# The first gate and up tiles of a transformer block fed with x times the scale, before the norm and the shift are known

## The chip, the cores and the metric

The kernel runs on one NeuronCore of one Trainium2 chip. The metric is the device time of one execution, in microseconds (us). Of the kernel before three executions were timed.

## The reference, cut to what matters

The reference is a residual block of several sublayers. Only its beginning matters here:

```
mod = (silu(c) @ w_ada + b_ada)            # 9 rows of 1024: shift, scale, gate of three sublayers
h   = rms_norm(x, g_ffn1) * (1 + sc1) + sh1
x   = x + 0.5 * gt1 * (silu(h @ w_gate) * (h @ w_up)) @ w_down
```

x is 512 tokens by 1024 channels in float32, w_ada is 1024 x 9216, the hidden width is 2816 (22 blocks of 128). After this come a mixer (mLSTM and dilated attention), a second feed-forward, and two more layers.

With g = g_ffn1 * (1 + sc1) and r = the reciprocal root of the mean square of a token, the first product is h @ W = r * ((x * g) @ W) + sh1 @ W. The left part needs neither r nor sh1 while TensorE works on it.

## The kernel before

Activations are kept transposed, channels on partitions: `xT` is 8 tiles (kt = 0..7) of 128 channels by 512 tokens. Each engine runs its own written-out program, in the order of the code; semaphores tie them together, and nothing is reordered by a planner.

Every weight tile passes the same pipeline, in a ring of four slots. SyncE loads it into `w_in` (the profile calls it w_stage; `load`, L477). ScalarE rounds it to `w_hi` (`hi`, L797). VectorE forms the remainder `w_lo` (`lo`, L1264) and raises `w_split`. TensorE then does three matmuls for each of the 8 channel tiles (`three`, L2034 to L2036: w_hi by h_hi, w_hi by h_lo, w_lo by h_hi), 24 in all for a tile of 128 outputs. The input h is split in the same way into `h_hi` (ScalarE) and `h_lo` (VectorE). Tiles 0 and 1 are the gate and the up columns of hidden block 0, tiles 2 and 3 those of block 1, and so on.

Before the first such matmul the kernel does this:

- SyncE loads the row of c, an identity, x, twenty small loads of norm weights, biases and `b_ada` (through L472), and then weight tiles 0 and 1; tiles 2 and 3 wait for `ada_done` 14.
- GpSimd loads 16 pieces of w_ada, each 128 rows by 1024 columns (512 KB, L546): 8 for the scale (q = 0), then 8 for the shift (q = 1), into the 8 buffers `ada_w`. Piece 8 + kt waits until VectorE has read piece kt.
- VectorE multiplies each piece by its part of silu(c) and adds it up (`ada_add`, L1274 and L1277). The sum still runs over 128 partitions. TensorE adds those up by 8 one-column matmuls with a vector of ones (`ada_reduce`, L2028), and VectorE adds b_ada (`ada_col`, L1283). `scale_cols` (L1289) then makes g, called `gs`.
- TensorE transposes x (L2001), ScalarE copies it to `xT` (L910) and squares it (L803), TensorE sums the squares (`norm_sum`, L2011), ScalarE makes `rs`, the r above (`norm_rs`, L834 and L836).
- `modulate` makes h: VectorE x * g * r (L1301), ScalarE h_hi with the shift as its bias (L859), VectorE h_lo (L1306).

TensorE's own order is: transposes of x, transposes of the constants' rows (L2005, L2006, which wait for the last small load), norm sums, `ada_reduce(0)`, `ada_reduce(1)`, then `project_pair` on tiles 0 and 1. The rest of w_ada (q = 2..8) is summed by VectorE in between the first feed-forward's tiles.

The second feed-forward and the mixer already begin on x times g, by `lead` (L2045 to L2057): one tile runs on x * g, and 8 one-column matmuls (L2055) multiply the same weights by the shift; VectorE multiplies the result by r afterwards, and the shift's part comes in as a bias.

Of the kernel before, what the change touches and what calls it, by code (L numbers as in the profile page):

```python
# [22 lines left out]
ALU = mybir.AluOpType  # L23
# [139 lines left out]
H_LEAD, H_NORM, H_EVEN, H_ODD = [None, 1, 3], [0, 2, 4], 5, 6  # L163


def read_by_lead(m, k):

    return ([None, 0, 1][m] * (KT - 1)) + k + 1
# [26 lines left out]
def build_program(nc, a, out):  # L195
    ctx = ExitStack()
    with ctx:
# [166 lines left out]
        x_rows = put("x_rows", [P, ST, D])  # L364
        ada_w = sb("ada_w", [P, KT, D])
# [15 lines left out]
        x_t, x_ready, silu_c = sem("x_t"), sem("x_ready"), sem("silu_c")  # L381
# [76 lines left out]
        def _(sp):  # L458
# [20 lines left out]
            def ffn(n):  # L479
                for half in range(2):  # L480
                    t0, f0 = T_FFN[n] + half * 3 * HALF, half * HALF
                    for j in range(2):
                        load(0, t0 + j, cols_of(w_gu[n], f0 * P + j * FF))
                    if t0 == 0:
                        sp.wait_ge(ada_done, 2 * KT - 2)

                    def pair_of_hidden(i):
                        for j in range(4):
                            if n == 1 and isinstance(i, int) and j == 2:
                                sp.wait_ge(shift_sum, 2)  # L490
                            load(i, t0 + 2 + j, cols_of(w_gu[n], i * (2 * P) + (f0 + 1 + j // 2) * P + j % 2 * FF))
# [10 lines left out]
            for n, (what, _, at) in enumerate(IN_TILES):  # L502
# [5 lines left out]
                else:  # L508
                    if n == RING:
                        sp.wait_ge(shift_sum, 1)  # L510
# [27 lines left out]
        def _(pool):  # L538
            pool.memset(rows[:], 0.0).then_inc(zeroed, 1)
            pool.memset(ones[:], 1.0).then_inc(zeroed, 1)  # L540
            pool.memset(eps[:], EPS).then_inc(zeroed, 1)

# [246 lines left out]
        def _(act):  # L789
            act.wait_ge(cols_t, 1)  # L790
            act.activation(cs[:], ps[7][:, 0:KT], ACT.Silu).then_inc(silu_c, 1)
# [35 lines left out]
            def norm_rs(n):  # L827
# [6 lines left out]
                act.activation(rs[:], ps[{0: 0, N_ODD: 3}.get(n, 1)][:], ACT.Ln, bias=eps[:], scale=1.0 / D).then_inc(ln_ready, 1)  # L834
# [16 lines left out]
            def modulate(m, shift):  # L851

                for kt in range(KT):
                    act.wait_ge(hn_ready, m * KT + kt + 1)
                    if m and kt < KT - 1:
                        act.wait_ge(pair_read, read_by_lead(m, kt))
                    elif m:
                        act.wait_ge(w_used, [None, T_MIX, T_FFN[1]][m] + 1)
# [3 lines left out]
            def ffn(n, norm_after, aside=None):  # L862
                for half in range(2):
                    t0, F0 = T_FFN[n] + half * 3 * HALF, (2 * n + half) * HALF

                    def hidden(i, f):


                        led = n == 1 and half == 0 and f == 0
                        for j in range(led, 2):  # L870
                            hi(i, t0 + 2 * f + 2 + j)
                        if led:
                            act.wait_ge(lead_ready, 2)
# [44 lines left out]
            act.wait_ge(gs_ready, 1)  # L918
# [220 lines left out]
            def odd_mixer():  # L1139
# [3 lines left out]
                for kt in range(KT):  # L1143
                    act.wait_ge(hn_ready, 3 * KT + kt + 1)
                    if kt < KT - 1:
                        act.wait_ge(pair_read, 2 * (KT - 1) + kt + 1)
# [104 lines left out]
        def _(dve):  # L1251
# [40 lines left out]
            def modulate(n, m, scale, shift):  # L1292
# [3 lines left out]
                dve.wait_ge(rs_ready, n + 1)  # L1296
                for kt in range(KT + 2):
                    if kt < KT:
                        if kt >= 4:
                            dve.wait_ge(h_ready, H_NORM[m] * KT + kt - 3)  # L1300
                        dve.scalar_tensor_tensor(hn[kt % 4], xT[:, kt], scale[:, kt:kt + 1], rs[:],  # L1301
                                                 ALU.mult, ALU.mult).then_inc(hn_ready, 1)
                    if kt >= 2:
# [22 lines left out]
            def ffn(n, sub, ada, aside=None):  # L1326
                for half in range(2):
                    t0, F0 = T_FFN[n] + half * 3 * HALF, (2 * n + half) * HALF

                    def hidden(i, f, q=None):  # L1330


                        for j in range(n == 1 and half == 0 and f == 0, 2):
# [6 lines left out]
                        dve.tensor_tensor(tmp2[:, f % 2], tmp[:, f % 2], ps[2 * (f % 2) + 1][:], ALU.mult) \  # L1340
                            .then_inc(prod_ready, 1)
# [53 lines left out]
            dve.wait_ge(silu_c, 1)  # L1395
            for q in range(2):
                for kt in range(KT):
                    ada_add(q, kt)
                    if q == 1 and kt == 0:
                        dve.wait_ge(cols_t, 2)  # L1400
                        dve.tensor_copy(cols[:], ps[1][:, 0:N_COLS]).then_inc(cols_ready, 1)
                        dve.wait_ge(cols_t, 3)
                        dve.tensor_copy(bada[:], ps[2][:, 0:72]).then_inc(cols_ready, 1)
                        dve.wait_ge(cols_ready, 2)
# [1237 lines left out]
```

## Time and profile before

| | us |
|---|---|
| median of three runs | 1562.89 (1562.22 to 1563.53) |
| time of the profiled execution | 1567.46 |
| its span, first to last instruction | 1565.8 |
| PE (TensorE matmul) busy | 1481.7 (95%) |
| PEld (TensorE weight load) busy | 1167.9 (75%) |
| DVE (VectorE) busy | 892.3 (57%) |
| ACT (ScalarE) busy | 616.3 (39%) |
| POOL (GpSimd) busy | 384.3 (25%) |
| mean granted TensorE clock | 0.982 of full |

Engines: PE is TensorE, PEld its weight loads, DVE VectorE, ACT ScalarE, POOL GpSimd, SP SyncE. In rows of the profile, `a<-b` is output from input; a float32 matmul that is not rounded to fp32r appears as two MATMUL entries. The profiled execution was 4.57 us longer than the median of the timed ones, and 1.66 us of its time lie outside the span.

### The profile page before, as it was taken

Reading aid. Unit: us, or ns where it says so; the run is one execution under the profiler, and the core shown is the slowest. Engines: PE = TensorE matmul, PEld = TensorE weight load, DVE = VectorE, ACT = ScalarE, POOL = GpSimd, SP = SyncE. Lnnn points to the kernel's source line nnn. Section 1 sums busy time; section 2 is a strip of 40 time slices with the busy share of each in tenths; the row PEclk is TensorE's granted clock in tenths of the full one; section 3 lists DMA queues with packets and bytes.
Section 4 is the critical chain, followed back from the end, with each engine's and each line's share of the span. In section 5 each row is a group of like instructions: output and inputs, shape, how many; then the busy total and the mean of one; then the engine's idle time right before and its main releaser. Section 6 shows DMA issues by size and latency. Waiting matters only on the chain. (4 is left out here: it accounts for less than half of the span.)

```text
span 1565.8 us, 19036 instructions
## 1 busy us (share of the span) xinstructions
PE 1481.7 (95%) x7032; PEld 1167.9 (75%) x7032; DVE 892.3 (57%) x1269; ACT 616.3 (39%) x928; POOL 384.3 (25%) x494
## 2 busy tenths in 40 slices
PE   5999999999999998999999999999899999988977
PEld 3788888888777776468888888888677787766555
DVE  5777436432763676737444344333566357799964
ACT  3422212232533454745342122223431245777634
POOL 3111001000000000040007788200102000999900
PEclk9999999999999999999999999999999999999978
DMA  9888526323242212023433423552133232222201
GB/s 348 269 273 271 198 68 215 94 87 106 70 138 67 81 54 66 1 58 85 121 86 113 138 81 123 160 205 85 54 95 108 68 97 82 81 78 71 68 27 55
DMA packets 204710, 177.93 MB, mean 114 GB/s; under 512 B 7379, under 2 KB 184079, under 8 KB 204118
## 3 DMA queue, kind: packets, MB, share of 16 engines
q1 hardware_dynamic: 188438, 121.87, 26.2%
q0 software_dynamic: 15040, 52.89, 9.6%
q10 hardware_dynamic: 1152, 2.10, 0.4%
q8 instruction: 51, 0.84, 0.2%
q14 instruction: 29, 0.24, 0.1%
HBM read 168.37 MB, written 8.46 MB: 113 GB/s over the span
## 5 line engine op out<-in xcount | busy, mean ns | idle before, releaser
L2034 PE MATMUL ps<-h_hi,w_hi 128*128 128x512 f32 x1224 | 490.7, 401 | 17.0 <-DVE w_lo L1264 11.2
L2036 PE MATMUL ps<-h_hi,w_lo 128*128 128x512 f32 x1224 | 477.9, 390 | 0.0
L2035 PE MATMUL ps<-h_lo,w_hi 128*128 128x512 f32 x1224 | 477.7, 390 | 0.0
L1264 DVE TENSOR_TENSOR w_lo<-w_stage,w_hi 128x1024 fp32r<-128x1024 f32 x225 | 295.3, 1326 | 220.2 <-ACT w_hi L797 217.7
L797 ACT ACTIVATE w_hi<-w_stage 128x1024 fp32r<-128x1024 f32 x225 | 230.7, 1048 | 189.8 <-PE ps L2036 183.4
L2034 PEld LDWEIGHTS ps<-h_hi,w_hi 128*128 128x128 f32 x1224 | 230.2, 188 | 86.1 <-issue 37.0
L2035 PEld LDWEIGHTS ps<-h_lo,w_hi 128*128 128x128 f32 x1224 | 230.5, 188 | 49.1 <-issue 3.6
L2036 PEld LDWEIGHTS ps<-h_hi,w_lo 128*128 128x128 f32 x1224 | 230.3, 188 | 49.2
L2034 PE MATMUL ps<-a_hi,w_hi 128*128 128x512 f32 x544 | 214.4, 394 | 13.1 <-DVE a_lo L1962 9.4
L2035 PE MATMUL ps<-a_lo,w_hi 128*128 128x512 f32 x544 | 212.8, 391 | 0.0
L2036 PE MATMUL ps<-a_hi,w_lo 128*128 128x512 f32 x544 | 212.8, 391 | 0.0
L1340 DVE TENSOR_TENSOR tmp<-tmp,ps 128x512 f32<-128x512 f32 x44 | 30.3, 688 | 197.0 <-PE ps L2036 196.9
L2034 PEld LDWEIGHTS ps<-a_hi,w_hi 128*128 128x128 f32 x544 | 102.8, 189 | 38.2 <-issue 14.0
L879 ACT ACTIVATE a_hi<-tmp 128x512 fp32r<-128x512 f32 (+1 forms) x44 | 27.9, 633 | 234.1 <-DVE tmp L1340 234.1
L2036 PEld LDWEIGHTS ps<-a_hi,w_lo 128*128 128x128 f32 x544 | 102.8, 189 | 21.8
L2035 PEld LDWEIGHTS ps<-a_lo,w_hi 128*128 128x128 f32 x544 | 102.9, 189 | 21.0
L546 POOL DMA_DIRECT2D ada_w<-in_w_ada x72 | 38.7, 539 | 226.6 <-DVE ada_acc L1274 118.9
L781 POOL TENSOR_TENSOR pacc<-pacc,tmp 128x512 f32<-128x512 f32 x49 | 74.4, 1519 | 63.3 <-ACT tmp L1215 59.4
L1277 DVE SCALAR_TENSOR_TENSOR ada_acc<-ada_w,cs,ada_acc 128x1024 f32<-128x1024 f32 x63 | 80.8, 1283 | 9.3 <-DMA ada_w<-in_w_ada 7.3
L1889 DVE SCALAR_TENSOR_TENSOR ps<-gb,cw,ps 128x512 f32<-128x512 f32 x110 | 74.3, 744 | 0.0
L781 POOL TENSOR_TENSOR pacc<-pacc,sq 128x512 f32<-128x512 f32 x48 | 71.9, 1499 | 3.9
L877 ACT ACTIVATE tmp<-ps 128x512 f32<-128x512 f32 x43 | 25.7, 599 | 108.8 <-PE ps L2036 108.8
(435 smaller groups left out, 1502.5 us busy)
## 6 DMA issues: line engine op xcount, KB each, us to landing
w_stage<-in_w_gu SPq DMA_DIRECT2D x88, 512.0 KB, 4.1
ada_w<-in_w_ada POOLq DMA_DIRECT2D x72, 512.0 KB, 6.7
w_stage<-in_w_down SPq DMA_DIRECT2D x44, 512.0 KB, 3.7
w_stage<-in_w_in SPq DMA_DIRECT2D x24, 512.0 KB, 3.9
w_stage<-in_odd_w_in SPq DMA_DIRECT2D x24, 512.0 KB, 3.7
w_stage<-in_even_w_in SPq DMA_DIRECT2D x16, 512.0 KB, 3.9
w_stage<-in_w_out SPq DMA_DIRECT2D x8, 512.0 KB, 3.8
mats<-mats_d POOLq DMA_DIRECT2D x4, 1024.0 KB, 7.0
```

What stands on the lines that cost most here:

```text
L546: pool.dma_start(ada_w[:, kt], a["w_ada"][0][kt * P:(kt + 1) * P, bass.ds(j * D, D)]) \
L781: pool.tensor_tensor(pacc[:, t % 2], pacc[:, t % 2], tap_of[m % 4], ALU.add).then_inc(pool_tap, 1)
L797: act.activation(w_hi[:, c % RING], w_in[:, c % RING], ACT.Copy).then_inc(w_hi_ready, 1)
L877: act.activation(tmp[:, f % 2], ps[2 * (f % 2)][:], ACT.Silu).then_inc(silu_ready, 1)
L879: act.activation(a_hi[:, bass.ds(i * (2 * S) + f * S, S)], tmp2[:, f % 2], ACT.Copy) \
L1264: dve.tensor_tensor(w_lo[:, c % RING], w_in[:, c % RING], w_hi[:, c % RING].bitcast(F32), ALU.subtract).then_inc(w_split, 1)
L1277: dve.scalar_tensor_tensor(acc, ada_w[:, kt], cs[:, kt:kt + 1], acc, ALU.mult, ALU.add).then_inc(ada_done, 1)
L1340: dve.tensor_tensor(tmp2[:, f % 2], tmp[:, f % 2], ps[2 * (f % 2) + 1][:], ALU.mult) \
L1889: dve.scalar_tensor_tensor(acc, gb[:, t % 2, k:k + S], cw[:, t, k:k + 1], acc, ALU.mult, ALU.add).then_inc(tap_done, 1)
L2034: pe.matmul(bank, w_hi[:, slot, k], rhs_hi, start=start, stop=False, skip_group_check=True)
L2035: pe.matmul(bank, w_hi[:, slot, k], rhs_lo, start=False, stop=False, skip_group_check=True)
L2036: return pe.matmul(bank, w_lo[:, slot, k], rhs_hi, start=False, stop=stop, skip_group_check=True)
```

## The change

- The pieces of w_ada for the scale wait for the first two small loads (`c_in`), and the pieces for the shift wait until the last piece of the scale has landed. The loads of weight tiles 0 and 1 wait until piece 5 of the scale has landed, tile 3 until piece 3 of the shift has, tiles 4 and 5 until the shift's matmuls (`shift_sum`) are done.
- VectorE sums only the scale's pieces, then makes `gs`.
- Tiles 0 and 1 run on x * g (`lead_pair`): ScalarE `scaled_hi`, VectorE `scaled_lo`, for each kt.
- The shift's pieces are summed on TensorE (`ada_rows`): float32 matmuls with `cs_wide` as the stationary operand (silu(c) in one column of 32, zeros in the others), four pieces at once in four groups of 32 output partitions, over two halves of 512 columns; 8 matmuls after kt = 3 and 8 after kt = 6. ScalarE copies the two banks to `ada_acc1`; then come `ada_reduce(1)` and 16 one-column matmuls of tiles 0 and 1 with the shift.
- Tiles 2 and 3 run as a pair on the full h. `modulate` runs for them, now while TensorE works on tiles 0 and 1 and after it.
- VectorE multiplies the results of tiles 0 and 1 by r, adds the shift's columns, and the product goes on as before.
- The rest renumbers semaphore values and places; the norm sum moves from bank 0 to bank 3.

The core of the diff:

```diff
+            def ada_rows(first):
+                for kt in range(first, first + 4):
+                    pe.wait_ge(ada_in[kt], 32)
+                for half in range(2):
+                    for g in range(4):
+                        mm = pe.matmul(ps[5 + half][32 * g:32 * g + 32, :], cs_wide[:, first + g],
+                                       ada_w[:, first + g, half * S:(half + 1) * S], start=(first == 0), stop=(first == 4),
+                                       skip_group_check=True)
+                mm.then_inc(ada_done, 4)
+            def lead_pair():
+                for k in range(KT):
+                    pe.wait_ge(h_ready, H_LEAD[0] * KT + k + 1)
+                    for j in range(2):
+                        if k == 0:
+                            pe.wait_ge(w_split, j + 1)
+                        mm = three(ps[j][:], j, k, h_hi[:, k], h_lo[:, k], k == 0, k == KT - 1)
+                        if k == KT - 1:
+                            mm.then_inc(w_used, 1)
+                    if k < KT - 1:
+                        mm.then_inc(pair_read, 1)
+                    if k == 3:
+                        ada_rows(0)
+                    if k == 6:
+                        ada_rows(4)
+                ada_reduce(1)
+                pe.wait_ge(mod_ready, 2)
+                for j in range(2):
+                    for k in range(KT):
+                        mm = pe.matmul(ps[7][:, KT + j:KT + j + 1], w_in[:, j, k], sublayer(0)[1][:, k:k + 1],
+                                       start=(k == 0), stop=(k == KT - 1))
+                mm.then_inc(shift_sum, 1)
...
             ada_reduce(0)
-            ada_reduce(1)
...
# GpSimd
-            for q in range(2):
-                for kt in range(KT):
-                    ada_load(q, ADA_ORDER[q], kt)
+            pool.wait_ge(c_in, 32)
+            for kt in range(KT):
+                ada_load(0, ADA_ORDER[0], kt)
+            pool.wait_ge(ada_in[KT - 1], 16)
+            for kt in range(KT):
+                ada_load(1, ADA_ORDER[1], kt)
# ScalarE
-            for c in range(2):
-                hi(0, c)
+            hi(0, 0)
+            act.wait_ge(gs_ready, 1)
+            scaled_hi(0, gs)
+            hi(0, 1)
+            for kt in range(1, KT):
+                scaled_hi(kt, gs)
             norm_rs(0)
+            hi(0, 2)
+            act.wait_ge(ada_done, 2 * KT)
+            for half in range(2):
+                act.activation(ada_acc1[:, half * S:(half + 1) * S], ps[5 + half][:], ACT.Copy).then_inc(c_ready, 1)
+            hi(0, 3)
             act.wait_ge(mod_ready, 2)
# VectorE, after the scale's ada_add, cols, bada and ada_col(0)
+            lo(0, 0)
+            scaled_lo(H_LEAD[0], 0, gs)
+            lo(0, 1)
+            for kt in range(1, KT):
+                scaled_lo(H_LEAD[0], kt, gs)
             modulate(0, 0, *sublayer(0))
+            dve.wait_ge(shift_sum, 1)
+            link(dve.tensor_copy(rcol[:, 0:2], ps[7][:, KT:KT + 2]))
+            dve.wait_ge(h_ready, (H_NORM[0] + 1) * KT)
+            dve.tensor_tensor(tmp[:, 0], ps[0][:], rs[:], ALU.mult).then_inc(lead_ready, 1)
+            dve.wait_ge(sq_used, KT)
+            dve.tensor_tensor(sq[:, 0], ps[1][:], rs[:], ALU.mult).then_inc(lead_ready, 1)
```

In `modulate` on VectorE, for this sublayer alone, `lo(0, 2)` stands ahead of the first x * g * r, and `ada_col(1)` and `lo(0, 3)` stand after the third; in the first hidden block no weight tile is split, so tiles 4 and 5 are split in the second.

## Rows read from the trace of the kernel before

**Rows 1.** The page, busy time of each engine over the span.
```profile
PE 1481.7 (95%) x7032; PEld 1167.9 (75%) x7032; DVE 892.3 (57%) x1269; ACT 616.3 (39%) x928; POOL 384.3 (25%) x494
```

**Rows 2.** Timeline of PE: start, duration, operation, idle before it and its releaser.
```profile
14.23 6.06 PE L2001 MATMUL ps<-ident,x_rows 128*128 128x128 f32 x32 [10.47 <-DMA x_rows<-in_x]
20.78 0.31 PE L2005 MATMUL ps<-ident,rows 103*128 103x103 f32 x1 [0.50 <-DMA rows<-in_b_ada]
...
20.99 7.90 PE L2011 MATMUL ps<-sq,ones 128*128 128x512 f32 x16
28.73 1.84 PE L2028 MATMUL ps<-ones,ada_acc 128*128 128x1 f32 x16
34.80 3.57 PE L2028 MATMUL ps<-ones,ada_acc 128*128 128x1 f32 x16 [4.23 <-DVE ada_acc L1277]
41.70 0.76 PE L2034 MATMUL ps<-h_hi,w_hi 128*128 128x512 f32 x1 [3.33 <-DVE h_lo L1306]
```

**Rows 3.** Timeline of DVE, the first 70 us.
```profile
21.02 1.28 DVE L1277 SCALAR_TENSOR_TENSOR ada_acc<-ada_w,cs,ada_acc 128x1024 f32<-128x1024 f32 x1 [0.24 <-DMA ada_w<-in_w_ada]
...
30.61 0.17 DVE L1283 TENSOR_TENSOR mod<-ps,bada 128x8 f32<-128x8 f32 x1 [0.62 <-PE ps L2028]
...
34.67 2.35 DVE L1264 TENSOR_TENSOR w_lo<-w_stage,w_hi 128x1024 fp32r<-128x1024 f32 x2
38.41 0.17 DVE L1283 TENSOR_TENSOR mod<-ps,bada 128x8 f32<-128x8 f32 x1 [1.39 <-PE ps L2028]
...
47.43 2.08 DVE L1306 SCALAR_TENSOR_TENSOR h_lo<-tmp,mod,h_hi 128x512 fp32r<-128x512 f32 x3
49.42 2.36 DVE L1264 TENSOR_TENSOR w_lo<-w_stage,w_hi 128x1024 fp32r<-128x1024 f32 x2
...
66.01 0.69 DVE L1340 TENSOR_TENSOR tmp<-tmp,ps 128x512 f32<-128x512 f32 x1 [1.54 <-PE ps L2036]
```

**Rows 4.** Windows of all engines: us, busy and count of PE, PEld, DVE, ACT, POOL, clock, DMA share, GB/s.
```profile
32.00:34.00 2.00, 0.00 (x0) 0.00 (x0) 1.82 (x2) 0.90 (x1) 0.00 (x0) 0.68 0.90 261
...
1553.70:1555.00 1.30, 1.30 (x12) 1.30 (x12) 0.00 (x0) 0.47 (x1) 0.00 (x0) 1.00 0.00 0
1555.20:1556.00 0.80, 0.80 (x4) 0.72 (x4) 0.00 (x0) 0.00 (x0) 0.00 (x0) 0.50 0.00 0
```

**Rows 5.** Windows of PE alone: us, busy and count, granted clock, DMA share, GB/s.
```profile
41.70:46.40 4.70, 4.70 (x11) 0.50 1.04 390
54.80:59.50 4.70, 4.70 (x22) 1.00 0.18 50
```

**Rows 6.** DMA queues from 5 to 13 us: packets, MB, share.
```profile
q1 hardware_dynamic: 496, 2.03, 62.5%
q0 software_dynamic: 361, 1.29, 39.8%
```

**Rows 7.** DMA queues from 14 to 31 us.
```profile
q0 software_dynamic: 1604, 5.84, 88.8%
q1 hardware_dynamic: 1604, 0.77, 15.6%
```

**Rows 8.** Timeline of ACT, the first 60 us.
```profile
25.69 0.61 ACT L910 ACTIVATE xT<-ps 128x512 f32<-128x512 f32 x1
...
31.84 1.06 ACT L797 ACTIVATE w_hi<-w_stage 128x1024 fp32r<-128x1024 f32 x1 [4.12 <-DMA w_stage<-in_w_gu]
...
55.85 0.63 ACT L879 ACTIVATE a_hi<-tmp 128x512 fp32r<-128x512 f32 x1 [0.88 <-DVE tmp L1340]
```

**Rows 9.** Groups of PE by line: count, busy us, mean ns, idle before.
```profile
L2508 PE MATMUL ps<-gb,dgc 128*128 128x512 f32 x34 | 14.9, 592 | 0.0
...
L2055 PE MATMUL ps<-mod,w_stage 128*128 128x1 f32 x16 | 1.8, 245 | 0.0
```

**Rows 10.** Timeline of PE in the attention.
```profile
646.46 1.95 PE L2302 MATMUL ps<-pt_a,va 128*64 128x256 f32 x16
```

More of the change, by code:

```diff
@@ L364, in build_program @@
         x_rows = put("x_rows", [P, ST, D])
+        put = region(at_of["a_lo"] + KT * S * 4, S * 4)
+        cs_wide = put("cs_wide", [P, KT, 32])
         ada_w = sb("ada_w", [P, KT, D])
@@ L509, in _ @@
                     if n == RING:
-                        sp.wait_ge(shift_sum, 1)
+                        sp.wait_ge(shift_sum, 2)
                     load(0, T_MIX + n, cols_of(a["w_in"][0], at))
@@ L541, in _ @@
             pool.memset(eps[:], EPS).then_inc(zeroed, 1)
+            pool.memset(cs_wide[:], 0.0).then_inc(zeroed, 1)
             def ada_load(q, j, kt):
@@ L833, in norm_rs @@
                     act.wait_ge(sq_used, SUMMED[n])
-                act.activation(rs[:], ps[{0: 0, N_ODD: 3}.get(n, 1)][:], ACT.Ln, bias=eps[:], scale=1.0 / D).then_inc(ln_ready, 1)
+                act.activation(rs[:], ps[{0: 3, N_ODD: 3}.get(n, 1)][:], ACT.Ln, bias=eps[:], scale=1.0 / D).then_inc(ln_ready, 1)
                 act.wait_ge(ln_ready, n + 1)
@@ L866, in hidden @@
                     def hidden(i, f):
-                        led = n == 1 and half == 0 and f == 0
-                        for j in range(led, 2):
+                        led = half == 0 and f == 0
+                        for j in range([2, 1][n] if led else 0, 2):
                             hi(i, t0 + 2 * f + 2 + j)
                         if led:
-                            act.wait_ge(lead_ready, 2)
+                            act.wait_ge(lead_ready, [1, 4][n])
                             act.activation(tmp[:, 0], tmp[:, 0], ACT.Silu, bias=rcol[:, 0:1]).then_inc(silu_ready, 1)
@@ L1296, in modulate @@
                 dve.wait_ge(rs_ready, n + 1)
+                if n == 0:
+                    lo(0, 2)
                 for kt in range(KT + 2):
@@ L1302, in modulate @@
                                                  ALU.mult, ALU.mult).then_inc(hn_ready, 1)
+                    if n == 0 and kt < 2:
+                        continue
+                    if n == 0 and kt == 2:
+                        ada_col(1, ADA_ORDER[1])
+                        lo(0, 3)
+                        dve.wait_ge(mod_ready, 2)
                     if kt >= 2:
@@ L1330, in hidden @@
                     def hidden(i, f, q=None):
-                        for j in range(n == 1 and half == 0 and f == 0, 2):
+                        led = half == 0 and f == 0
+                        for j in range([2, 1][n] if led else 0, 2):
                             lo(i, t0 + 2 * f + 2 + j)
@@ L1967, in _ @@
             modulate(2, 2, *sublayer(2))
-            dve.wait_ge(shift_sum, 2)
+            dve.wait_ge(shift_sum, 3)
             link(dve.tensor_copy(rcol[:, 0:1], ps[7][:, 0:1]))
@@ L2010, in norm_sum @@
                 pe.wait_ge(sq_ready, n * KT + kt + 1)
-                pe.matmul(ps[0][:], ones[:], sq[:, kt % 2], start=(kt == 0), stop=(kt == KT - 1)) \
+                pe.matmul(ps[3][:], ones[:], sq[:, kt % 2], start=(kt == 0), stop=(kt == KT - 1)) \
                     .then_inc(sq_used, 1)
@@ L2025, in ada_reduce @@
                 pe.wait_ge(ada_done, q * KT + KT)
+                if isinstance(q, int) and q == 1:
+                    pe.wait_ge(c_ready, 4)
                 upto(pe, mod_ready, q)
@@ L2074, in hidden @@
                     def hidden(i, f):
+                        if t0 == 0 and f == 1 and isinstance(i, int) and i == 0:
+                            project_pair(2, H_NORM[0] * KT, 2)
+                            return
                         if n == 1 and half == 0 and f == 1 and isinstance(i, int) and i == 0:
```

78 lines of the change are left out of this document (40 added, 38 removed).

## Prediction

> **What bounds the kernel now.** I read the page's busy times first: TensorE is busy for 95% of the span [rows 1], so only what lets TensorE start its stream of matmuls earlier, or what is put into that stream, can move the end. Next the timeline of TensorE over the first 42 us. Its first real matmul of weights starts at 41.70; before it stand the transposes of x (14.23), the constants' rows (20.78), the norm sums (20.99), the reduction of the scale (28.73 to 30.57) and, after 4.23 us of idling for the shift's last sum, that of the shift (34.80 to 38.37) [rows 2]. From 41.70 it does not stop: 11 matmuls take the first 4.70 us and the other 85 of tiles 0 to 3 follow at 0.227 us, so tile 4 starts at about 65.7, which fits VectorE's product for block 1 at 66.01 [rows 3, 5]. That instant is my yardstick: behind it both kernels run the same work at the bound of TensorE, so the change is worth what tile 4's start moves by. Last the windows for the clock: granted 1.00 until past 32 us, then half (0.50) until about 46.4 [rows 4, 5]; 11 matmuls in 4.70 us against 22 at full clock, so that the low level costs the stream 2.3 us.
>
> **The head, up to the first matmul.** What is removed is the wait for the shift: two reductions become one, and 41.70 no longer hangs on VectorE's eighth shift sum (end at about 34.7), `lo` of two tiles (2.35), `ada_col` (38.41) and the first x * g * r. What is left ahead is the chain of x. In 8 us x (q1) moved 2.03 MB and w_ada (q0) 1.29 MB [rows 6]. Held back by `c_in`, the pieces of w_ada come about 2 us later, in which x gets the 0.41 MB/us of both instead of 0.25; x should land about 1 us earlier, and in no case more than 3 (2.1 MB at 0.41 is 5 us). The last small load, which ended at 20.78, still shares its queue with w_ada's stream and gains 0.5 to 1 us. The norm sums and the reduction behind it (9.8 us from 20.78 to 30.57) keep their length, as `ada_reduce(0)` still stands behind them in TensorE's order: its end moves from 30.57 to 29.8. The scale's last piece was added by 22.3 already [rows 3], so bringing the scale earlier buys nothing by itself. Then, on VectorE: `ada_col` and `gs` 0.4, `lo` of tile 0 1.2, `scaled_lo` 0.7 (the 0.66 step of h_lo) [rows 3]: TensorE starts at 32.1. ScalarE's `scaled_hi` (0.6) and `hi` of tile 1 (1.06) [rows 8] lie beside these. `lo` of tile 1 ends at 33.3, so tile 1's first matmul waits 0.6 us. The start is 9.6 us earlier.
>
> Is the data there? Tiles 0 and 1 are asked for at about 18 us, behind the constants. While w_ada streams (q0) the hardware queue q1, which carries the weights, got 0.77 MB in 17 us (0.045 MB/us) against 5.84 MB [rows 7]. Between the scale's end (about 20) and the shift's first bytes (about 22.3) the weights have the engines alone, at some 0.3 MB/us: 0.7 MB of the 1.05 MB of two tiles. The rest takes 6 to 8 us at the low rate: tile 1 lands at 28.5 to 30, ahead of ScalarE's turn at 31. The shift's 4.2 MB at 0.34 are in by 35, ahead of both `ada_rows`.
>
> **Tiles 0 and 1 with the shift's sums.** 48 matmuls at 0.227 are 10.9 us; with the stall they end at 43.5 at full clock. `ada_rows` has 16 matmuls of 512 columns in float32. One such matmul with a full array costs 0.88 us (17 of them, 34 entries, in 14.9) [rows 9]: 14.0 us one after another. With two column halves, two at a time were no dearer than one: 8 matmuls of 256 columns took 1.95 us in the attention, where one by one they would take 3.5 [rows 10, 9]. No row has four groups. The bounds are 3.5 us (all four side by side) and 14.0 (none); two at a time give 7.0. I take 4.0, with some draining between the two shapes, since the pair shows that separate groups do run together. The Trainium skill's page "TensorE: Matmul & The Clock Gate", in its part on packing small matmuls, has three column tiles of this size at 2.38 times the speed and four row tiles at 3.07; an estimate by the latter would be 4.6 us. No run here shows it.
>
> The clock: before, TensorE did one-column matmuls from 28.73, idled from 30.57, and was at half by 33 us [rows 2, 4]. Now the same work stands in front of a gap of 2.3 us. One-column work doesn't seem to hold the clock up: at 1553.70 to 1555.00 TensorE was busy throughout with it, at full clock, and just after it was at half [rows 4]. So the clock falls here too; it is half for some 3.5 us of the lead, which costs 1.8 (bounds 0 and 3). Lead and shift sums end at 43.5 + 4.0 + 1.8 = 49.3. The same page says in its part on the clock gate that the low clock is the default and activity releases it; by that rule as by these rows, the new stretch below is where the change pays.
>
> **What now stands between tile pairs.** This is new on TensorE's path, and before it was idle time ahead of the start: the eight matmuls of `ada_reduce(1)`, 1.9 (ScalarE's two copies of the sums, 1.2, lie beside the last six matmuls of the pair, 1.4); the way over VectorE's `ada_col` and back, 0.3 (0.17 and two semaphores); 16 one-column matmuls with the shift, 3.6 (eight are 1.8) [rows 9]. Together 5.8 us in which hardly a column is streamed. At half clock eight cost 3.57 instead of 1.84 [rows 2]. I expect the clock to fall in the middle of it: 1.5 for the rest of these small matmuls and 2.3 for the first 4.7 us of the next pair, as at 41.70 [rows 5]. Bounds: 0 and 6. Tiles 2 and 3 start at 49.3 + 5.8 + 1.5 = 56.6 and end at 56.6 + 10.9 + 2.3 = 69.8.
>
> **What is late next.** `ada_col(1)` at 51.5 frees VectorE: `lo` of tile 3, then 13 steps of 0.66 for h, some 9.9 us; the products with r 0.8; ScalarE's silu 0.7, VectorE's product 0.75, ScalarE's a_hi 0.63, `hi` of tile 4 1.06, VectorE's `lo` 1.2 [rows 3, 8]: 15.4 us with the handovers, tile 4 ready at 66.9. Behind the waiting instructions of both engines only this chain is queued. It is hidden while the clock falls (69.8 is later) but ends the stage if it does not. h_lo comes every 1.32 us, TensorE takes 1.36: no loss. The load of tile 4 starts after `shift_sum` and has 8 us. The other edits (numbers of semaphores, bank 3, the zeroing of `cs_wide`, two tiny silus) lie in front of x's landing or change no instruction's length: 0.
>
> **The sum.** Earlier start -9.6; stall for tile 1 +0.6; `ada_rows` +4.0; reduction, way and shift matmuls +5.8; clock before 2.3, now 1.8 + 1.5 + 2.3 = 5.6, so +3.3: +4.1 us, tile 4 at 69.8 against 65.7. On the profiled execution's 1567.46 (span 1565.8, 1.66 outside) that is 1571.6; the difference is carried to the median, 1562.89 + 4.1 = 1567.0.
>
> **The rivals.**
> - *The clock holds between the pairs.* For it: no row before has one-column work of this kind within the warm stream, so its effect is inferred from the end of the kernel. Against it: the row at 1555 and a stretch three times as long. Then 66.0, but tile 4 waits for its `lo` until 66.9: +1.2, 1564.1. If it holds in the lead too, tile 4 is ready at 65.1: -0.6, 1562.3.
> - *The column groups don't run four abreast.* Two at a time: +3.0 more, 1570.0; none: +10, 1577.
> - *x and the constants come much sooner* (the other side). Mechanism: with w_ada held back x lands up to 3 us earlier, the small loads with it, and the transposes, norm sums and reduction all move by that. Before x had to share from its first byte. Against it: the last small load landed 6.5 us after x, whose transposes start at 14.23, amid w_ada's stream [rows 2], which is still there. From a shift of 3 us, with the clock holding between the pairs, the kernel is faster: -3.5, 1559.4.
> - *Tile 1's weights are late.* If the weights get only 0.3 MB ahead of the shift, tile 1 lands at about 34: +2 to +3, 1569.5. The change would then have moved the wait from VectorE to the queue.
>
> **Chances and range.** The forecast 0.40 (its own range 1565 to 1570); clock holds 0.27; groups not abreast 0.13; much sooner 0.13; weights late 0.07. A difference under 0.2%, 3.1 us, can't be told from none: the limits are 1559.8 and 1566.0. Faster: the sooner case, 0.13, and a little of the second, 0.15. Same: most of the second and a quarter of the forecast, 0.34. Slower: 0.51. The range 1560 to 1572.5 leaves out most of the sooner case's half and the case of no packing.
>
> **What would show it.** The first weight matmul at 32 (a step of the head is wrong if it is off by over 1.5); the norm sums' start at 20 and the reduction's end at 29.8; 16 entries of `ada_rows` in 1.8 to 2.2 us; a reduction and 32 entries of shift matmuls between the pairs with the clock at 0.5 in part of them; tile 4 at 69.8, with no wait of TensorE for w_lo there. A wait for w_lo there instead of a low clock would make the first rival right; the forecast is wrong as a whole if tile 4 starts before 63 or if the later stream has changed.

## Result and profile after

| | before | after |
|---|---|---|
| median of eight runs each, us | 1562.93 (1560.10 to 1563.56) | 1567.62 (1564.75 to 1568.69) |
| profiled execution, us | 1567.46 | 1565.67 |
| its span, us | 1565.8 | 1564.0 |
| granted clock, mean | 0.982 | 0.987 |

The ratio after to before is 1.0031, with a 95% interval of 1.0022 to 1.0040: 4.7 us slower. The same kernel, timed again beside the experiments, gave 1.0035 (1.0023 to 1.0048).

The two profiled executions seem to say the opposite, since the one of after is the shorter. They are single executions, and the one of before was 4.5 us above its own median. Whole spans can't be compared here; places in the stream can. One mark is VectorE's `w_lo` of the same weight tile, the 21st it splits and the 201st. Timeline of VectorE, before:

```profile
150.06 1.23 DVE L1264 TENSOR_TENSOR w_lo<-w_stage,w_hi 128x1024 fp32r<-128x1024 f32 x1
...
1347.90 1.88 DVE L1264 TENSOR_TENSOR w_lo<-w_stage,w_hi 128x1024 fp32r<-128x1024 f32 x1
```

The same view of after:

```profile
154.83 1.23 DVE L1282 TENSOR_TENSOR w_lo<-w_stage,w_hi 128x1024 fp32r<-128x1024 f32 x1
...
1347.76 1.88 DVE L1282 TENSOR_TENSOR w_lo<-w_stage,w_hi 128x1024 fp32r<-128x1024 f32 x1
```

At the 21st tile after is 4.8 us behind, and it stays so until about 498 us. Then the profiled execution of before, a slower one than its median, loses those microseconds by its clock. In the windows 620 to 640, 640 to 690 and 1100 to 1120 us TensorE was granted 0.83, 0.97 and 0.91 of the full clock before, and 0.91, 1.00 and 1.00 after, a difference of 4.9 us of work. The repeated profile of the changed kernel (e0 below) was granted 0.83, 0.97 and 0.91, as before, and its 201st tile is at 1352.44, 4.5 us behind. So the loss is made in the first 90 us, and what follows differs from one execution to the next.

The page of after, busy times:

```profile
PE 1485.7 (95%) x7096; PEld 1170.9 (75%) x7096; DVE 889.5 (57%) x1272; ACT 622.2 (40%) x939; POOL 384.7 (25%) x495
```

TensorE is busy for 4.0 us more than in [rows 1], with two blocks of `ada_rows` and the shift's small matmuls. Its timeline in the head, to set beside [rows 2]:

```profile
11.35 6.23 PE L2038 MATMUL ps<-ident,x_rows 128*128 128x128 f32 x32 [7.57 <-DMA x_rows<-in_x]
18.09 0.31 PE L2042 MATMUL ps<-ident,rows 103*128 103x103 f32 x1 [0.51 <-DMA rows<-in_b_ada]
...
18.30 7.90 PE L2048 MATMUL ps<-sq,ones 128*128 128x512 f32 x16
26.04 1.84 PE L2067 MATMUL ps<-ones,ada_acc 128*128 128x1 f32 x16
30.33 0.79 PE L2073 MATMUL ps<-h_hi,w_hi 128*128 128x512 f32 x1 [2.45 <-DVE h_lo L1349]
...
37.52 1.92 PE L2104 MATMUL ps<-ada_w,cs_wide 128*32 128x512 f32 x16
...
43.72 1.92 PE L2104 MATMUL ps<-ada_w,cs_wide 128*32 128x512 f32 x16
...
47.09 1.84 PE L2067 MATMUL ps<-ones,ada_acc 128*128 128x1 f32 x16
49.18 5.66 PE L2129 MATMUL ps<-mod,w_stage 128*128 128x1 f32 x32 [0.26 <-DVE mod L1301]
54.70 0.77 PE L2073 MATMUL ps<-h_hi,w_hi 128*128 128x512 f32 x1
...
67.03 0.39 PE L2073 MATMUL ps<-h_hi,w_hi 128*128 128x512 f32 x1
...
77.68 0.39 PE L2075 MATMUL ps<-h_hi,w_lo 128*128 128x512 f32 x1
79.70 2.05 PE L2067 MATMUL ps<-ones,ada_acc 128*128 128x1 f32 x16 [1.63 <-DVE ada_acc L1295]
```

The first weight matmul is at 30.33 instead of 41.70, and the pair of tiles 2 and 3 starts at 54.70. Tile 4 starts at 67.03; before it was at 65.74. So only 1.3 us are lost up to there. The last row is the one to see: the reduction of the third sum (q = 2) waits 1.63 us for VectorE. The same instruction before had no wait:

```profile
76.63 1.84 PE L2028 MATMUL ps<-ones,ada_acc 128*128 128x1 f32 x16
```

In after, TensorE's matmul ahead of the reduction starts at 77.68, and in the stream the next would have followed 0.227 later, at 77.91. The wait costs 1.8 us, and the lag is 3.1 us at 79.70. The windows of TensorE of after (us, busy and count, granted clock, DMA share, GB/s) show where the last 1.7 us go:

```profile
47.00:50.00 3.00, 2.74 (x26) 1.00 0.91 298
50.00:54.00 4.00, 4.00 (x24) 0.59 0.87 332
54.00:57.00 3.00, 3.00 (x10) 0.50 0.29 86
...
60.00:76.00 16.00, 16.00 (x72) 1.00 0.90 274
76.00:80.00 4.00, 2.37 (x13) 1.00 0.89 280
80.00:84.00 4.00, 4.00 (x21) 0.68 0.95 296
84.00:88.00 4.00, 4.00 (x18) 0.90 1.02 347
```

Behind the wait the clock falls once more: 0.68 over four microseconds and 0.90 over the next four, where before it was full. That is 0.32 * 4 + 0.10 * 4 = 1.7 us of work not done. 1.3 + 1.8 + 1.7 is the 4.8 of the mark at 154.83. VectorE's timeline shows why its sums were late; compare [rows 3]:

```profile
27.99 0.17 DVE L1301 TENSOR_TENSOR mod<-ps,bada 128x8 f32<-128x8 f32 x1 [5.24 <-PE ps L2067]
...
48.97 0.17 DVE L1301 TENSOR_TENSOR mod<-ps,bada 128x8 f32<-128x8 f32 x1 [7.68 <-PE ps L2067]
49.05 1.22 DVE L1282 TENSOR_TENSOR w_lo<-w_stage,w_hi 128x1024 fp32r<-128x1024 f32 x1
...
56.80 2.08 DVE L1332 SCALAR_TENSOR_TENSOR h_lo<-tmp,mod,h_hi 128x512 fp32r<-128x512 f32 x3
...
62.87 1.23 DVE L1282 TENSOR_TENSOR w_lo<-w_stage,w_hi 128x1024 fp32r<-128x1024 f32 x1 [0.26 <-ACT w_hi L807]
...
69.79 0.68 DVE L1372 TENSOR_TENSOR tmp<-tmp,ps 128x512 f32<-128x512 f32 x1
...
76.98 2.67 DVE L1295 SCALAR_TENSOR_TENSOR ada_acc<-ada_w,cs,ada_acc 128x1024 f32<-128x1024 f32 x2
79.56 0.68 DVE L1372 TENSOR_TENSOR tmp<-tmp,ps 128x512 f32<-128x512 f32 x1
```

The last group of h_lo ends at 58.9 instead of 49.5 in [rows 3]. From 48.97 on VectorE never waits for TensorE, only for short handovers of ScalarE. The product at 66.01 waited 1.54 us for TensorE before; now, at 69.79, it waits for nothing, since TensorE finished that pair of tiles 2.8 us earlier, at 67.0. Before, the last two pieces of the third sum were added from 73.22 and ended at 75.9, 0.7 us ahead of the reduction at 76.63. Now they end at 79.65. That margin of 0.7 us is what the change used up. The row of before, in VectorE's timeline:

```profile
73.22 2.67 DVE L1277 SCALAR_TENSOR_TENSOR ada_acc<-ada_w,cs,ada_acc 128x1024 f32<-128x1024 f32 x2
```

### The profile page after: what moved, and what is told of

Read it like the earlier page. It is cut to its first block and busy times, and to the rows that moved or that the text cites. A ratio compares the mean times of both kernels' runs of the same rounds, so it can differ in the third digit from the quotient of the medians.

```text
span 1564.0 us, 19190 instructions
## 1 busy us (share of the span) xinstructions
PE 1485.7 (95%) x7096; PEld 1170.9 (75%) x7096; DVE 889.5 (57%) x1272; ACT 622.2 (40%) x939; POOL 384.7 (25%) x495
## 5 line engine op out<-in xcount | busy, mean ns | idle before, releaser
L2075 PEld LDWEIGHTS ps<-h_hi,w_lo 128*128 128x128 f32 x1224 | 230.7, 188 | 49.5
L2073 PE MATMUL ps<-a_hi,w_hi 128*128 128x512 f32 x544 | 213.8, 393 | 13.1 <-DVE a_lo L1999 9.4
L1295 DVE SCALAR_TENSOR_TENSOR ada_acc<-ada_w,cs,ada_acc 128x1024 f32<-128x1024 f32 x56 | 71.8, 1282 | 2.5 <-DMA ada_w<-in_w_ada 0.8
```

Source lines behind the costliest of these rows:

```text
L1295: dve.scalar_tensor_tensor(acc, ada_w[:, kt], cs[:, kt:kt + 1], acc, ALU.mult, ALU.add).then_inc(ada_done, 1)
L2073: pe.matmul(bank, w_hi[:, slot, k], rhs_hi, start=start, stop=False, skip_group_check=True)
L2075: return pe.matmul(bank, w_lo[:, slot, k], rhs_hi, start=False, stop=stop, skip_group_check=True)
```

## Experiments

All have the changed kernel as their base unless the text says otherwise. The ratio is to the kernel before, timed with them on the same chip. The expectations weigh two theories: V, that the loss is made by VectorE's chain and TensorE's wait for it, and P, that it is made by what now stands on TensorE's own path. "Mark" is the start of `w_lo` of the 21st tile in the profile (before 150.06, after 154.83).

### e0_changed: the changed kernel again

No edit.

> The changed kernel again, beside its variants. Both theories: +4.7 us on the kernel before (ratio 1.003). Theory V (VectorE's chain): from ada_col(1) at about 49 us VectorE works without a pause until its last sum of q = 2 at 79.7; TensorE waits there about 2 us, and its clock is at half for one stretch soon after (81 to 85 us). Theory P (TensorE's path): the loss is the one-column stretch between the pairs and the low clock in it; the wait near 78 us is a by-product. By both the wait and both low stretches should be in this profile too.

Median 1569.57, ratio 1.0035 (1.0023 to 1.0048); mark 154.55. Its PE timeline:

```profile
79.41 1.95 PE L2067 MATMUL ps<-ones,ada_acc 128*128 128x1 f32 x16 [1.64 <-DVE ada_acc L1295]
```

The wait is no accident of one execution. Here the 4.5 us at the mark come with 5.5 by the ratio. e1, e2 and e3 were timed with it.

### e1_short_sums: the third sum made short

```diff
+                    n = 64 if isinstance(q, int) and q == 2 else D
-                    dve.tensor_scalar(acc, ada_w[:, 0], cs[:, 0:1], ...
+                    dve.tensor_scalar(acc[:, 0:n], ada_w[:, 0, 0:n], cs[:, 0:1], ...
...
# the same for the other pieces
```

> Leaves out part of the computation: VectorE's eight sums of q = 2 run over 64 of 1024 columns (about 0.1 us each instead of 1.28). Theory V: the wait of 2.0 us before ada_reduce(2) and the low clock behind it (1.7 us) go: 3.7 us less than the changed kernel, +1.0 on the kernel before. Theory P: no change against the changed kernel (+4.7), or at most the 2.0 us of the wait.

Median 1564.24, ratio 1.0008 (0.9998 to 1.0017); mark 151.53. PE timeline:

```profile
78.11 1.84 PE L2069 MATMUL ps<-ones,ada_acc 128*128 128x1 f32 x16
```

No wait, and the clock is 1.00 from 78 to 88 us. That is 4.2 us less than the changed kernel by the ratios (0.0027 of 1563), 3.0 to 3.3 by the marks. The wait of one instruction and the clock behind it are most of the result, as theory V expected (+1.0 on the kernel before; measured +1.3, between -0.3 and +2.7). It doesn't yet show a way out, because work was left out.

### e2_split_early: two of VectorE's steps moved ahead of the shift

`hi` and `lo` of tile 3, and the fourth x * g * r, stand before the wait for the shift.

```diff
                 if n == 0:
                     lo(0, 2)
+                    lo(0, 3)
+                    for kt in range(4):
+                        scaled(kt)          # x * g * r
+                    ada_col(1, ADA_ORDER[1])
...
-                        ada_col(1, ADA_ORDER[1])
-                        lo(0, 3)
```

> The whole computation: hi and lo of tile 3 and the fourth x * g * r stand ahead of ada_col(1), where both engines idle. VectorE's chain from ada_col(1) gets shorter by 1.15 + 0.66 = 1.8 us. Theory V: TensorE's wait before ada_reduce(2) falls from 2.0 to 0.2 us, 1.8 us less than the changed kernel, and 3.5 less if the clock holds behind it. Theory P: TensorE's work is unchanged, no gain (+4.7).

Median 1566.51, ratio 1.0018 (1.0008 to 1.0028); mark 153.43. PE timeline:

```profile
78.27 1.95 PE L2079 MATMUL ps<-ones,ada_acc 128*128 128x1 f32 x16 [0.78 <-DVE ada_acc L1295]
```

Half of the wait goes, where 0.2 us was expected to be left, and the clock still falls behind it (80 to 84 us: 0.65). At the mark the gain is 1.1 us, about the length of the wait saved; by the ratios it is 2.7.

### e3_shift_in_pair: the shift's matmuls behind the first channel of the next pair

```diff
                 ada_reduce(1)
-                pe.wait_ge(mod_ready, 2)
-                for j in range(2):
-                    for k in range(KT):
-                        mm = pe.matmul(ps[7][:, KT + j:KT + j + 1], w_in[:, j, k], ...
...
+                    if k == aside_at:        # 1, in the pair of tiles 2 and 3
+                        shift_of_lead()
```

> The whole computation: the 16 one-column matmuls of tiles 0 and 1 with the shift stand after channel tile 1 of the pair of tiles 2 and 3 instead of ahead of it. The pair starts at about 51 instead of 54.7, as its h_lo is ready then; tile 4 starts 1.5 to 3 us earlier (64 to 65.5 instead of 67), where VectorE's w_lo of tile 4 at about 64 allows it. Theory V: ada_reduce(2) still waits for VectorE until about 79.7, so the wait grows by what the pair gained and the time stays within 0.5 us of the changed kernel. Theory P: 1.5 to 3 us less than the changed kernel.

Median 1568.60, ratio 1.0030 (1.0018 to 1.0041); mark 155.29: no gain. PE timeline, then VectorE's:

```profile
50.94 0.62 PE L2073 MATMUL ps<-h_hi,w_hi 128*128 128x512 f32 x1 [2.15 <-DVE h_lo L1332]
...
55.35 4.45 PE L2130 MATMUL ps<-mod,w_stage 128*128 128x1 f32 x32
...
70.32 0.39 PE L2073 MATMUL ps<-h_hi,w_hi 128*128 128x512 f32 x1
...
81.74 1.95 PE L2067 MATMUL ps<-ones,ada_acc 128*128 128x1 f32 x16 [0.37 <-DVE ada_acc L1295]
```

```profile
64.90 1.23 DVE L1282 TENSOR_TENSOR w_lo<-w_stage,w_hi 128x1024 fp32r<-128x1024 f32 x1 [1.24 <-ACT w_hi L807]
```

The pair starts 2.9 us earlier than in e0 (53.84), but tile 4 starts at 70.32, 3.6 us later than in e0 (66.73), where 64 to 65.5 was expected. The shift's matmuls cost 4.45 us inside the pair, and the clock was granted 0.50 from 60 to 64 us and 0.90 from 64 to 68, where it was full in e0. So TensorE's own path became longer. VectorE's chain became longer too: the slot of tile 4 is free only when the shift's matmuls are done, so its load and `w_lo` come 2.0 us later than in after (64.90 against 62.87). TensorE waits 0.37 us for the third sum instead of 1.64, and the clock behind it stays full (80 to 100 us), which gives back nearly what the path lost. The run doesn't decide between the two theories, since its condition, an earlier tile 4, didn't come about.

### e4_early_sums: e2, and two pieces of the third sum added before the shift is there

```diff
+                    dve.wait_ge(ada_done, 2 * KT)
+                    for kt in range(2):
+                        ada_add(2, kt)
                     ada_col(1, ADA_ORDER[1])
```

> The whole computation: e2_split_early, and VectorE sums the first two pieces of q = 2 ahead of ada_col(1), in its idle time. The chain from ada_col(1) is shorter by 1.8 + 0.75 + 1.28 = 3.8 us. Theory V: no wait of TensorE before ada_reduce(2) is left, and no low clock behind it: 3.7 us less than the changed kernel, +1.0 on the kernel before, as with the short sums. Theory P: no gain.

Median 1565.21, ratio 1.0016 (1.0004 to 1.0028); mark 150.56. PE timeline:

```profile
77.13 1.84 PE L2083 MATMUL ps<-ones,ada_acc 128*128 128x1 f32 x16
```

Complete work, no wait, clock 1.00 from 78 to 88: at the mark only 0.5 us behind before, and 4.0 ahead of the changed kernel. By the ratios the gain is 3.0 us (3.7 expected by theory V, none by theory P), and 2.5 remain against before (0.6 to 4.4). The trace explains 0.5 of those 2.5; where the rest is, if there is one, stays open.

### e5_short_all: e1, and two of the sixteen shift matmuls

```diff
                 for j in range(2):
-                    for k in range(KT):
-                        mm = pe.matmul(ps[7][:, KT + j:KT + j + 1], w_in[:, j, k], ...
+                    mm = pe.matmul(ps[7][:, KT + j:KT + j + 1], w_in[:, j, 0], ...
```

> Leaves out parts of the computation: the short sums of e1, and 2 of the 16 one-column matmuls with the shift. This prices TensorE's path between the pairs once VectorE's sums are out of the way. The pair of tiles 2 and 3 then starts at h_lo, about 51 us instead of 54.7, and ends at 62 to 64; tile 4 can start when its w_lo is ready, about 15 us after ada_col(1), at 64. Theory V: 2 to 3 us less than with the short sums alone, bound by w_lo of tile 4, which TensorE waits for: -1 to -2 on the kernel before. Theory P: the full 3.6 to 5 us of the matmuls and their low clock come back: -2.5 to -4.

Median 1561.53, ratio 0.9992 (0.9983 to 1.0002); mark 148.29. PE timeline:

```profile
48.80 0.61 PE L2130 MATMUL ps<-mod,w_stage 128*128 128x1 f32 x4 [0.26 <-DVE mod L1303]
50.68 0.77 PE L2075 MATMUL ps<-h_hi,w_hi 128*128 128x512 f32 x1 [1.28 <-DVE h_lo L1334]
...
63.85 0.47 PE L2075 MATMUL ps<-h_hi,w_hi 128*128 128x512 f32 x1 [0.45 <-DVE w_lo L1282]
```

With VectorE relieved, what TensorE saves does reach the mark: 3.2 us less than e1. By the ratio the kernel is 1.3 us faster than before (between 2.7 faster and 0.3 slower), which fits theory V (1 to 2 faster) and not theory P (2.5 to 4). Then tile 4 waits for its `w_lo`: 63.85 is the bound that the prediction put 15.4 us behind the start of `ada_col(1)`. It holds: `mod` at 48.58 plus 15.3.

### e6_one_group: the sums of the shift in one group of columns

All sixteen entries of an `ada_rows` go to output partitions 0 to 31.

```diff
-                        mm = pe.matmul(ps[5 + half][32 * g:32 * g + 32, :], cs_wide[:, first + g],
+                        mm = pe.matmul(ps[5 + half][0:32, :], cs_wide[:, first + g],
```

> All matmuls of ada_rows go to one group of 32 output partitions, one behind the other; ScalarE copies rows that hold other values, so the sum is wrong by them. The same 16 matmuls. If four groups run abreast in the changed kernel, each ada_rows takes 7.0 us instead of 1.9, and the kernel is 10.2 us slower than the changed one. If the groups were not what makes them short (a matmul with 32 columns of weights being cheap by itself), the time stays. Theory V: the wait before ada_reduce(2) stays the same 2 us, as ada_col(1) moves with the rest. Theory P: the same 10 us.

Median 1578.54, ratio 1.0103 (1.0079 to 1.0127). PE timeline:

```profile
36.76 7.05 PE L2104 MATMUL ps<-ada_w,cs_wide 128*32 128x512 f32 x16
```

The second block, at 48.04, took the same. 7.05 against 1.92 us is a factor of 3.67: in the changed kernel all four groups run at nearly the same time. Twice the difference is 10.3 us, and the run is 9.0 us above the median of e0, taken on another chip (the marks differ by 9.7, the ratios by 10.6). The rival "the column groups don't run four abreast" is out.

### e7_reduce_early: e4, with the scale's reduction ahead of the last norm sums

```diff
                 norm_sum(0, kt)
-            pe.wait_ge(x_ready, KT)
-            pe.wait_ge(cols_ready, 2)
-            ada_reduce(0)
+                if kt == 4:
+                    pe.wait_ge(x_ready, KT)
+                    pe.wait_ge(cols_ready, 2)
+                    ada_reduce(0)
...
# ScalarE: hi(0, 0) and scaled_hi(0, gs) ahead of the last square
# the shift's matmuls of tile 0 between the pairs, those of tile 1 behind the first channel of the next pair
```

> The whole computation, all three parts: e4_early_sums; the 8 matmuls of tile 0 with the shift stay between the pairs, those of tile 1 go behind the first channel tile of the next pair; ada_reduce(0) stands behind the fifth norm sum, and ScalarE scales x tile 0 ahead of its last square. The first weight matmul comes 2 to 2.8 us earlier than in the changed kernel (at 27.5 to 28.3), the pair of tiles 2 and 3 starts 2 us sooner after ada_col(1). Theory V and P together (VectorE's chain shortened first, TensorE's path then counting): 3.7 + 2.4 + 2 = 8 us less than the changed kernel, 3 us less than the kernel before, more if the clock falls for a shorter time. If VectorE's chain still bounds, only 2.4 + 3.7: -1.3 on the kernel before.

Median 1563.68, ratio 1.0003 (0.9992 to 1.0015); mark 150.42. PE timeline:

```profile
22.97 1.95 PE L2086 MATMUL ps<-ones,ada_acc 128*128 128x1 f32 x16 [0.37 <-ACT xT L922]
...
46.69 1.95 PE L2150 MATMUL ps<-mod,w_stage 128*128 128x1 f32 x16 [0.59 <-DVE mod L1304]
...
50.57 3.41 PE L2150 MATMUL ps<-mod,w_stage 128*128 128x1 f32 x16
...
76.99 1.84 PE L2086 MATMUL ps<-ones,ada_acc 128*128 128x1 f32 x16
```

It ties with the kernel before, where 3 us less was expected. The reduction of the shift comes 2 us earlier than in e4, but the reduction of q = 2 stands where it stood. The gain in the head was given back between the pairs: the granted clock was 0.52 from 49 to 54 us and 0.54 from 54 to 60, which is 5.2 us of work not done; in e4 it was 3.4 (50 to 54: 0.54, 54 to 57: 0.50, 57 to 60: 0.97).

### e8_no_hold: the scale's pieces not held back

```diff
-            pool.wait_ge(c_in, 32)
```

> The changed kernel, but the pieces of w_ada for the scale don't wait for the first two small loads (the wait on c_in is gone). x landed 2.9 us earlier in the changed kernel (transposes at 11.35 instead of 14.23), where the prediction gave this wait 1 us. If the wait is what did it: transposes back at 13.5 to 14.3, the first weight matmul and all behind it 2.2 to 2.9 us later, and the kernel 2 to 3 us slower than the changed one (+7 to +8 on the kernel before). If something else did it (the later loads of the weight tiles): x lands as in the changed kernel and the time stays.

Median 1570.68, ratio 1.0055 (1.0038 to 1.0072); mark 157.93, 3.4 us behind the changed kernel in e0. PE timeline:

```profile
14.21 5.08 PE L2037 MATMUL ps<-ident,x_rows 128*128 128x128 f32 x32 [10.53 <-DMA x_rows<-in_x]
...
32.77 0.79 PE L2072 MATMUL ps<-h_hi,w_hi 128*128 128x512 f32 x1 [2.45 <-DVE h_lo L1348]
```

The transposes of x are back at 14.2, as in [rows 2]. So the whole shift of the head, 2.9 us, is the hold of w_ada and not the later loads of the weight tiles. The lag of 3.4 us on e0 is there at the end of the lead already (reduction at 50.20 against 46.80) and stays. With x not earlier at all the first weight matmul is at 32.77; the prediction's chain behind the constants gives 32.9 for that case, so that part of it was well sized.

### e9_shift_rows: e4, with the shift streamed through the weights

The shift's column becomes the stationary operand, as silu(c) is in `ada_rows`, and the weights stream: 8 matmuls of 256 columns in four groups. ScalarE copies the rows out, and two one-column matmuls behind channel tile 4 of the next pair add the groups up. A third piece of q = 2 is also summed early.

```diff
-                for j in range(2):
-                    for k in range(KT):
-                        mm = pe.matmul(ps[7][:, KT + j:KT + j + 1], w_in[:, j, k], ...
+                for k in range(KT):
+                    g = k % 4
+                    mm = pe.matmul(ps[5][32 * g:32 * g + 32, 0:2 * P], cs_wide[:, k], w_in[:, 0:2, k],
+                                   start=(k < 4), stop=(k >= 4), skip_group_check=True)
```

> The whole computation: e4_early_sums with three pieces of q = 2 summed ahead; and the shift's product with tiles 0 and 1 is made with the shift as the stationary operand, in one column of 32, and the weights streamed: 8 matmuls of 256 columns in four groups side by side (about 0.9 us instead of 5.3), then a copy by ScalarE and 2 one-column matmuls behind channel tile 4 of the next pair. The next pair starts when its h_lo is ready, 1.6 us after ada_col(1), at about 50 instead of 53.7. Theory V and P: VectorE's chain is 26.4 us from ada_col(1), so ada_reduce(2) can start at about 74.5 (77.1 with the early sums alone, 79.7 in the changed kernel): 2.5 us less than e4_early_sums, 0 to -1.5 on the kernel before.

Median 1564.65, ratio 1.0021 (1.0011 to 1.0031); mark 151.84. PE timeline:

```profile
50.13 1.07 PE L2150 MATMUL ps<-w_stage,cs_wide 128*32 128x256 f32 x16 [0.53 <-DVE cs_wide L1334]
...
66.28 0.47 PE L2094 MATMUL ps<-h_hi,w_hi 128*128 128x512 f32 x1 [1.28 <-DVE w_lo L1286]
...
78.30 1.95 PE L2088 MATMUL ps<-ones,ada_acc 128*128 128x1 f32 x16 [0.90 <-DVE ada_acc L1299]
```

VectorE's timeline:

```profile
60.83 0.16 DVE L1467 COPY rcol<-ps 128x2 f32<-128x2 f32 x1 [1.93 <-PE ps L2157]
```

The shift matmuls fall from 5.66 us in after to 1.07. What is saved is spent in two waits for VectorE, 1.28 at tile 4 and 0.90 at the reduction. The kernel is 3.3 us slower than before, where 0 to 1.5 faster was expected. VectorE is late because it waits itself: the two one-column matmuls stand behind channel tile 4 of the pair and run at 60.29, and VectorE, which needs them for the products of tiles 0 and 1, waits 1.93 us for them. Its chain from `ada_col(1)` to tile 4's `w_lo` was 15.1 us long, 13.1 in e4. The clock also fell once more between the pairs (0.75 from 50 to 54 us, 0.76 from 54 to 57), and x landed about 1 us later than in e4 (transposes at 11.94 against 10.92). Behind the wait of 0.90 us the clock stayed full this time, up to 100 us.

### e10_rows_early: e9 with the early reduction of e7

The eighth norm sum moves behind channel tile 1 of the first pair as well, and ScalarE does the first two `hi` and the first `scaled_hi` ahead of the last square.

```diff
-            for kt in range(KT):
+            for kt in range(KT - 1):
...
+                    if k == 1:
+                        norm_sum(0, KT - 1)
```

> The whole computation: e9_shift_rows, with ada_reduce(0) behind the fifth norm sum, the eighth norm sum behind channel tile 1 of the first pair, and ScalarE's first scaled tile and hi of tile 1 ahead of its last square. ada_reduce(0) ends at 24.9 instead of 27, the first weight matmul stands at 27.5 to 28.5 (29.3 to 30.3 before), and all behind it moves by 1.5 to 2 us, VectorE's chain too: 1.5 to 2 us less than e9_shift_rows, -2 to -4 on the kernel before. If the clock falls during the norm sums, as it did with the early reduction alone, 1 us of it is lost.

Median 1562.84, ratio 1.0002 (0.9993 to 1.0012); mark 148.79. PE timeline:

```profile
61.62 0.47 PE L2095 MATMUL ps<-h_hi,w_hi 128*128 128x512 f32 x1 [1.28 <-DVE w_lo L1287]
...
73.64 1.95 PE L2089 MATMUL ps<-ones,ada_acc 128*128 128x1 f32 x16 [0.89 <-DVE ada_acc L1300]
```

Tile 4 starts at 61.62, 4.1 us earlier than before, and waits there. The first weight matmul is at 27.27, VectorE waits only 0.33 us for the shift's columns, and from 47 to 60 us, between the pairs and in the next one, the clock is 1.00 throughout, as in no other complete version here. At the mark the kernel is 1.3 us ahead of before: the wait of 0.89 us and a fall of the clock behind it (74 to 78 us: 0.84, 78 to 82: 0.73) stand in between. By the time it ties with the kernel before, where 2 to 4 us less was expected. It is 5.2 us faster than the changed kernel by the ratios. e7 and e10 are the best complete versions, not to be told apart by their times; none beat the kernel before.

## Why the prediction was right, and where it was not

The total was right: +4.1 us predicted, +4.7 measured, in the range and in its likeliest case, "slower by over 0.2%". Its parts were not all right. Two errors of about the same size cancelled, and that they did is luck.

- **x and the constants.** Predicted 1 us earlier, at most 3; measured 2.9 (14.23 to 11.35), and 2.7 for the last small load (20.78 to 18.09). This was the step that the third rival sized correctly. The hold by `c_in` delays the first issue of w_ada from 1.49 to 3.78 us, but from 4 to 8 us its queue moved only 0.03 MB while x moved 1.50; in e8 it was 0.64 against 0.96. x had the engines nearly alone for about 4 us, not the 2 us of the delay. e8 shows that the hold is the cause. The rival's other condition, a clock that holds between the pairs, failed. Its price, -3.5, doesn't follow from the prediction's own terms: x 3 us earlier is 2.2 us more than the 0.8 in the sum, which with the first rival's prices makes -1.0, or -2.8 if the clock holds in the lead too.
- **The head's other steps.** The reduction behind the norm sums stayed in its place, 7.74 us behind their start as before, and what follows took 4.29 us from it to the first weight matmul, much as reckoned. `lo` of tile 1 and its load cost nothing visible in after; in e0 there was a wait of 0.17 us. The rival "tile 1's weights are late" is out.
- **`ada_rows`.** 2.0 us each taken, 1.92 measured, 3.84 together. The estimate from the Trainium skill's page "TensorE: Matmul & The Clock Gate" (part 3, on packing small matmuls), 4.6 for both, was too high. e6 gives 3.67 as the factor of four column groups, more than the 2.38 of three which that page has.
- **The clock in the lead.** 1.8 us taken; seven matmuls at 0.43 us and a mixed one cost 1.6. The lead with its sums ended at 47.09, predicted 49.3. The difference is the head's: the start 1.8 us earlier than predicted and no stall of 0.6 us.
- **Between the pairs.** Reduction 1.84 (1.9), way 0.25 (0.3), shift with its low clock 5.52 (3.6 + 1.5), the low clock of the next pair 1.4 (2.3). The mechanism was right: the clock fell (0.59) although TensorE was busy throughout 50 to 54 us. The rival "the clock holds between the pairs" is out. Against the prediction the lead ended 2.2 us earlier, the stretch was 0.3 longer and the next pair 0.9 shorter: tile 4 started at 67.0, predicted 69.8.
- **What is late next.** This is the step that failed. The prediction followed VectorE's chain to tile 4's `w_lo` (15.4 us from `ada_col(1)`; measured 15.1 in after: 48.97 to 64.10), found it hidden, and stopped there, because "behind it both kernels run the same work at the bound of TensorE". But that chain goes on: split of tiles 5 to 7 and eight pieces of the third sum, until 79.65, and TensorE needs that sum 10.9 us after tile 4 starts. Before it had 0.7 us to spare. The change started VectorE's chain for tile 4 5.4 us later (62.87 against 57.5) while TensorE came only 1.3 later. The wait cost 1.8 us and its low clock 1.7. e1 shows it by taking the sum away (-4.2 us), e4 by complete work (-3.0 by the ratios, -4.0 at the mark).

The yardstick, tile 4's start, was therefore wrong: it moved by 1.3 us where the time moved by 4.7. The sum came out because the head and the lead gained 2.2 us more than predicted and the next pair lost 0.9 less, against 3.5 us that were not foreseen: 4.1 - 2.8 + 3.5 = 4.8. Had every step up to tile 4 been sized right, the forecast would have been +1.3 us, which the prediction counts as "same", and out by 3.4.

Why the change brings nothing even without that wait: TensorE starts 11.4 us earlier, and spends 3.8 us on `ada_rows` with some 0.4 of draining around them, 7.6 on reduction, way and shift matmuls, and 1.6 + 1.4 on the low clock, which cost 2.3 before: 12.5 us, a little more than it gained. What is left to win there is the shift matmuls, and e9 and e10 win them; but tile 4 then waits for VectorE, whose chain (ready at 64.1 in after) stands only 2.9 us ahead of TensorE's.

## What to carry to other kernels

When work of one engine is moved under another's stream, follow the moved engine's queue to its next join with the stream, and to the one after that: here the join that decided stood 10.9 us behind the place where the sum stopped, with a margin of 0.7 us. A short wait of TensorE can cost more than its own length, by the clock behind it: in after the wait cost 1.8 us and the clock 1.7, in e10 0.89 and 1.7; in e9, with a wait of 0.90, the clock did not fall. So remove such a wait wholly rather than shorten it, and read the clock behind it each time. Compare two profiles by the start of the same instruction at several places, not by their spans.

## What the runs showed of the hardware

- From the issue of w_ada at 3.78 us to its first usable piece (VectorE starts on it at 11.40) were 7.6 us, while the stream of x ran. Between 4 and 8 us its queue moved 0.03 MB. Issued at 1.49 (before), the first piece was usable at 5.90, 4.4 us later.
- Four float32 matmuls into four groups of 32 output partitions ran 3.67 times as fast as in one group (7.05 and 1.92 us for 16 entries of 512 columns). 16 entries of 256 columns took 1.07.
- While TensorE was 100% busy with one-column matmuls its granted clock fell: window 50 to 54 us at 0.59, 54 to 57 at 0.50. The same product with the weights streamed (e9) took 1.07 us instead of 5.66; with it the clock in these two windows was 0.75 and 0.76 in e9, and 1.00 in both in e10.
- Behind the wait for the third sum the clock fell in after (wait 1.63 us, then 0.68 from 80 to 84), in e2 (0.78, then 0.65 from 80 to 84) and in e10 (0.89, then 0.59 from 76 to 80), not in e9 (0.90) and e3 (0.37), nor without a wait (e1, e4). What decides at 0.8 to 0.9 us stays open.
- The lower clock appears in single executions also where the kernels do the same (640 to 690 us: 0.97 and 1.00), which moved the same mark of the changed kernel's two profiles by 5 us (201st tile at 1347.76 and 1352.44, 21st at 154.83 and 154.55).
